# Column products of the FFN and MLP: two matrix instructions merged into one of 512 columns, the row factor applied at the residual

## What is computed

```
rms_norm(h, g) = h * rsqrt(mean(h * h) + eps) * g        # a factor per row, a gain per column
MLP:  h = h + square(relu(rms_norm(h, g) @ w_in)) @ w_out          # hidden width 4096, 2 times
FFN:  gate, up = split(rms_norm(h, g) @ w_gate_up)                 # hidden width 2816, 8 times
      h = h + 0.5 * ((silu(gate) * up) @ w_down)
```

## Time and profile before

| | before |
|---|---|
| three runs | 2901.33, 2904.25, 2906.99 us |
| median | 2904.25 us |
| span of the profiled execution | 2897.5 us |
| TensorE busy (matmul) | 2740.8 us, 95% |
| VectorE busy | 1697.9 us, 59% |
| ScalarE busy | 1285.5 us, 44% |
| mean granted TensorE clock | 0.969 |

### The profile page before, as it was taken

The page is one execution under the profiler, slowest core; times in us unless marked ns, Lnnn a source line. Parts: engine busy times, 40 slices in busy tenths (PEclk is TensorE's granted clock), DMA queues, the critical chain, the costliest instruction groups (busy, mean ns, idle before and its releaser), DMA issues.

```text
span 2897.5 us, 44300 instructions
## 1 busy us (share of the span) xinstructions
PE 2740.8 (95%) x18332; PEld 2491.1 (86%) x18342; DVE 1697.9 (59%) x1903; ACT 1285.5 (44%) x1376; POOL 6.8 (0%) x17
## 2 busy tenths in 40 slices
PE   7899998998999989999988999999799999998998
PEld 6689886997999869999976799999679999986997
DVE  6665576656555546565555455655655565564555
ACT  5443454334434544443433434444444444355433
POOL 0000000000000000000000000000000000000000
PEclk9899998999999999999998999999899999998999
DMA  7245432554454325545432255454315545541452
GB/s 270 87 177 189 174 139 82 194 191 148 162 189 165 139 84 184 194 174 187 179 139 80 101 189 189 175 188 170 115 45 201 179 171 201 184 153 70 163 185 73
DMA packets 63473, 454.85 MB, mean 157 GB/s; under 512 B 7104, under 2 KB 7360, under 8 KB 8848
## 3 DMA queue, kind: packets, MB, share of 16 engines
q1 hardware_dynamic: 61920, 448.82, 42.7%
q0 software_dynamic: 1024, 3.51, 0.3%
q10 hardware_dynamic: 432, 1.13, 0.1%
HBM read 452.38 MB, written 1.05 MB: 156 GB/s over the span
## 4 chain that ended last, share of the span: by engine, by line
PE 87%; DVE 6%; ACT 4%; issue 1%; DMA 1%; SPq 0%; DVEq 0%; ACTq 0%
PE tb L226 14%; PE tb L229 14%; PE tb L228 14%; PE acc L257 11%; PE acc L258 10%; PE acc L259 10%; DVE w_lo L206 2%; PE acc L226 1%; PE acc L228 1%; PE acc L229 1%; ACT w_hi L199 1%; PE tb L634 1%; PE tb L288 1%; PE acc L664 1%; PE tb L632 1%
## 5 line engine op out<-in xcount | busy, mean ns | idle before, releaser
L206 DVE TENSOR_TENSOR w_lo<-raw,w_hi 128x2048 fp32r<-128x2048 f32 x426 | 973.8, 2290 | 477.6 <-ACT w_hi L199 477.6
L199 ACT ACTIVATE w_hi<-raw 128x2048 fp32r<-128x2048 f32 x426 | 811.6, 1910 | 582.6 <-PE tb L229 302.9
L226 PE MATMUL tb<-xT,w_hi 128*128 128x256 f32 x3520 | 1004.0, 285 | 15.0 <-DVE w_lo L206 12.4
L228 PE MATMUL tb<-xT,w_hi 128*128 128x256 f32 x3520 | 997.4, 283 | 0.0
L229 PE MATMUL tb<-xT,w_lo 128*128 128x256 f32 x3520 | 997.2, 283 | 0.0
L226 PEld LDWEIGHTS tb<-xT,w_hi 128*128 128x128 f32 x3520 | 676.4, 192 | 24.4 <-DVE w_lo L206 8.1
L228 PEld LDWEIGHTS tb<-xT,w_hi 128*128 128x128 f32 x3520 | 676.6, 192 | 4.5
L229 PEld LDWEIGHTS tb<-xT,w_lo 128*128 128x128 f32 x3520 | 676.6, 192 | 0.0
L257 PE MATMUL acc<-w_hi,cat 128*128 128x512 f32 x1152 | 453.1, 393 | 10.1 <-DVE cat L674 6.5
L258 PE MATMUL acc<-w_hi,cat 128*128 128x512 f32 x1152 | 450.7, 391 | 0.0
L259 PE MATMUL acc<-w_lo,cat 128*128 128x512 f32 x1152 | 449.4, 390 | 0.0
(11 more groups left out here) (260 smaller groups left out, 2427.3 us busy)
## 6 DMA issues: line engine op xcount, KB each, us to landing
raw<-in_stream SPq DMA_DIRECT2D x426, 1024.0 KB, 4.8
h<-in_x SPq DMA_DIRECT2D x2, 512.0 KB, 4.9
gain<-in_gains POOLq DMA_DIRECT2D x2, 512.0 KB, 9.3
xn<-in_gates POOLq DMA_DIRECT2D x2, 512.0 KB, 8.4
out<-xn SPq DMA_DIRECT2D x2, 512.0 KB, 2.7
cst<-in_consts ACTq DMA_DIRECT2D x1, 960.5 KB, 12.5
big<-in_pT POOLq DMA_DIRECT2D x2, 256.0 KB, 3.0
gain<-in_gains POOLq DMA_DIRECT2D x1, 320.0 KB, 3.6
```

Source lines behind the costliest of these rows:

```text
L199: act.activation(w_hi[:, k % SPLIT, :], raw[:, k % RAW, :], ACT.Copy).then_inc(hi_done, 1)
L206: dve.tensor_tensor(w_lo[:, k % SPLIT, :], raw[:, k % RAW, :], w_hi[:, k % SPLIT, :], ALU.subtract).then_inc(lo_done, 1)
L226: pe.matmul(dst(f), hi, src[:, kt, 0, :], start=kt == 0 and (after is None or f == 0), stop=False, skip_group_check=after is not None)
L228: pe.matmul(dst(f), hi, src[:, kt, 1, :], start=False, stop=False, skip_group_check=after is not None)
```

## The change

`up` keeps high and low input side by side (they lie so in `xT`). For each tile and step it issues one instruction of 512 columns, high weights times both inputs, and one of 256 columns, low weights times the high input, behind the first half: two instructions where there were three. Each tile now has a PSUM bank of its own, high products in columns 0 to 255, low ones in 256 to 511, so a chunk fills two banks. ScalarE copies the second half out of both banks (new), VectorE adds it to the first half (in the MLP this add takes the place of the product with `rb`; in the FFN both sums are new, the gate is then still multiplied by `rb`, the up half no longer). The row factor of the up half, or its square in the MLP, goes into `residual` as a factor per row, with the 0.5. There is no second set of banks: TensorE waits for the sum of a pair before it overwrites its banks, and the first chunk of a phase goes to `acc` banks 0 and 2, so `zero_acc` now waits for the first sum.

```diff
-        def up(pe, c, bank, i=0, after=None):
-            columns(pe, c, lambda f: tb[:, bank, f * SEQ:(f + 1) * SEQ], 2, KT, SEQ, i, after=after)
+        def up(pe, c, banks, i=0, after=None):
...
+            for f, kt in order:
+                at = kt * SEQ + f * P
+                hi, lo = w_hi[:, s, at:at + P], w_lo[:, s, at:at + P]
...
+                both = xT[:, kt, :, :].rearrange("p a t -> p (a t)")
+                if kt == 0:
+                    pe.matmul(banks[f], hi, both, start=True, stop=False)
+                last = pe.matmul(banks[f][:, 0:SEQ], lo, xT[:, kt, 0, :], start=False, stop=False)
+                if kt:
+                    last = pe.matmul(banks[f], hi, both, start=False, stop=kt == KT - 1)
+            last.then_inc(chunk_used, 1)
+
+        UP_FIRST = [acc[:, 0, :], acc[:, 2, :]]
+        UP_0, UP_1 = [tb[:, b, :] for b in (0, 1)], [tb[:, b, :] for b in (2, 3)]
...
         def mlp_pe(pe, l, c, n):
-            up(pe, c, 0, after=x_ready(pe, n))
+            up(pe, c, UP_FIRST, after=x_ready(pe, n))
             if l == 0:
                 pe.wait_ge(*when("zeroed", 0))
+            pe.wait_ge(hid_v, base + 1)
             zero_acc(pe, c)
-            spread(pe, n)
...
-                    up(pe, c + 1 + 2 * j, (j + 1) % 3, i)
+                    pe.wait_ge(hid_v, base + 1 + j + 3 * i)
+                    up(pe, c + 1 + 2 * j, UP_0, i)
...
         def mlp_dve(dve, l, c, n):
...
-                by_rb(dve, two(f_up), two(tb[:, k % 3, :]), n, k == 0).then_inc(hid_u, 1)
+                dve.wait_ge(hid_b, bb + 1 + k + 3 * i)
+                dve.tensor_tensor(two(f_up), up_part(k or None, 0, 0), two(f_bu), ALU.add).then_inc(hid_v, 1)
...
         def ffn_pe(pe, f, c, n):
-            up(pe, c, 0, after=x_ready(pe, n))
-            zero_acc(pe, c)
-            up(pe, c + 1, 1)
-            spread(pe, n)
+            up(pe, c, UP_FIRST, after=x_ready(pe, n))
+            up(pe, c + 1, UP_1)
+            spread(pe, n, 0)
+            pe.wait_ge(hid_p, bg + 1)
+            zero_acc(pe, c)
+            pe.wait_ge(*when("rb", n))
...
+                    pe.wait_ge(hid_p, bg + 1 + j + 2 * i)
+                    up(pe, c + 2 + 3 * j, UP_0, i)
+                    pe.wait_ge(hid_v, base + 1 + j + 2 * i)
+                    up(pe, c + 3 + 3 * j, UP_1, i)
...
         def ffn_act(act, f, c, n):
...
+            low_gate(0, 0)
             split_hi(act, c, SPLIT)
-            hidden(0)
+            low_up(0, 1)
             split_hi(act, c, 1 + SPLIT)
+            spread_act(act, n, "ffn")
+            gate(0)
+            hidden(0)
...
         def ffn_dve(dve, f, c, n):
...
                     split_lo(dve, c, 3 + 3 * j + SPLIT, i)
+                    hidden_lo(j + 1, i)
+                    split_lo(dve, c, 4 + 3 * j + SPLIT, i)
...
-            residual(dve, n, c + CHUNKS_FFN - 1, 0.5)
+            residual(dve, n, c + CHUNKS_FFN - 1, row_scale)
...
-                    if last_kind != "bridge":
+                    if last_kind not in ("bridge", "ffn"):
                         split_lo(dve, c, -2 + SPLIT)
```

More of the change, by code:

```diff
@@ L186, in write @@
         cf = small[:, 226:228]
+        row_scale = small[:, 236:238]
         dots = small[:, 228:232]
@@ L328, in spread_act, with spread @@
         def spread_act(act, n, kind):
-            if kind not in ("ple", "bridge", "end"):
+            if kind not in ("mlp", "ple", "bridge", "end"):
                 act.wait_ge(*when("spread", n))
-                act.activation(rb, tb[:, 3, 0:SEQ], ACT.Copy).then_inc(*sig("rb", n))
-        def spread(pe, n):
+                act.activation(rb, tb[:, 0 if kind == "ffn" else 3, 0:SEQ], ACT.Copy).then_inc(*sig("rb", n))
+        def spread(pe, n, bank=3):
             pe.wait_ge(*when("diag", n))
-            pe.matmul(tb[:, 3, 0:SEQ], every, diag, start=True, stop=True).then_inc(*sig("spread", n))
+            pe.matmul(tb[:, bank, 0:SEQ], every, diag, start=True, stop=True).then_inc(*sig("spread", n))
         def newton(dve, root, mean, a, b, out_, key):
@@ L368, in factor_dve @@
             newton(dve, rms, ms, r0, r1, rstd, n)
+            if kind == "mlp":
+                dve.tensor_tensor(row_scale, rstd, rstd, ALU.mult).then_inc(*sig("own", (n, "scale")))
+                dve.wait_ge(*when("own", (n, "scale")))
+            if kind == "ffn":
+                dve.tensor_scalar(row_scale, rstd, 0.5, None, ALU.mult).then_inc(*sig("own", (n, "scale")))
+                dve.wait_ge(*when("own", (n, "scale")))
             if kind == "ple":
                 dve.nop().then_inc(*sig("rstd", n))
+            elif kind == "mlp":
+                pass
             elif kind not in ("bridge", "end"):
@@ L395, in x_ready, with residual @@
             return after
-        def residual(dve, n, c_last, scale=1.0):
+        def residual(dve, n, c_last, scale=None):
             for nn in range(2):
@@ L426, in down @@
                  acc_done=c if last else None, before_last=before_last)
-        def up(pe, c, bank, i=0, after=None):
-            columns(pe, c, lambda f: tb[:, bank, f * SEQ:(f + 1) * SEQ], 2, KT, SEQ, i, after=after)
+        def up(pe, c, banks, i=0, after=None):
+            pe.wait_ge(lo_done, c + 1 + RAW * i)
+            s = c % SPLIT
+            order = [(f, kt) for f in range(2) for kt in range(KT)]
+            if after is not None:
+                order.sort(key=lambda step: step[1])
+            for f, kt in order:
+                at = kt * SEQ + f * P
+                hi, lo = w_hi[:, s, at:at + P], w_lo[:, s, at:at + P]
+                if after is not None and f == 0:
+                    after(kt)
+                both = xT[:, kt, :, :].rearrange("p a t -> p (a t)")
[5 more added lines that the diff above has]
+            last.then_inc(chunk_used, 1)
```

117 lines of the change are left out of this document (72 added, 45 removed).

## The result

| | before | after |
|---|---|---|
| runs | 14 | 14 |
| median | 2903.20 us | 2910.02 us |
| lowest to highest | 2897.75 to 2906.99 us | 2907.80 to 2913.39 us |
| span of the profiled execution | 2897.5 us | 2911.6 us |

The ratio is 1.002, 95% interval 1.0013 to 1.0028: slower by 0.2%, 6.8 us, where 7 us faster was forecast. The time lies in the range and on the wrong side of no change.

A forecast was written before the change was run, and what follows sets the result against it. TensorE's pace was taken to bound the ten phases, other engines counting only at phase ends. A 43.3 us gain against waits of 11.2, 15.2 and 9.6 took 2904.25 to 2897 us, range 2884 to 2920.

The forecast's parts named there:

- The three waits: TensorE waits: 1.6 us at 7 FFN ends, 1.9 us at 8 FFN starts, 5.2 us idle at 2 MLP starts.
- the last pair's hidden low part: FFN end: ready about 5.6 us after its column product, wanted after 5.4; the 0.2 us lies under the residual wait.
- the sum: Whole kernel: -43.3 gain, +11.2 FFN ends, +15.2 FFN starts, +9.6 MLP starts, together -7.3 us.
- No wait inside the loops: Steady pairs in the loops: new copies and adds cost nothing more; TensorE waiting for sums there would show the forecast wrong.
- B: FFN starts: the clock falls at each, about 1.6 us more per FFN, 12.8 us, giving 2910 us; chance 0.14.
- C: Column products: a narrow instruction costs less behind a wide one, step 0.340 us, gain 66.6 us, time 2874 us; chance 0.08.
- the clock in the MLP: MLP starts: lower clock after the idle time loses 1.5 us each, bounds 0 and 2.5, 2 times.
- Gain 0.013 us a step, 43.3 us: Column products through `up`: 3328 steps lose one instruction each, a step falling from 0.360 to 0.347 us.
- columns plus 0.013: Matrix instructions at full clock: time is the columns' time plus 0.013 us, so 0.2267 us for 512 columns.
- D: Column products: the wide instruction on `xT` costs more than in the row product; slower, 2930 or 2963 us; chance 0.12.
- the estimate from it: Removed instructions: 2.5 ns fixed part each gives back 8.3 us, time 2932 us; no chance beyond D's.
- the first case: Whole kernel: the sum holds within its bounds, 2890 to 2903 us; chance 0.60.

The follow-up runs named there:

- the second profile: The changed kernel profiled once more with no edit, on one chip; 2910.35 us.
- The side by side: The kernel before and the changed kernel, each profiled once more with no edit and compared stage by stage; 2903.86 and 2910.35 us.
- the grouped kernel: Against the changed kernel with all three border moves: in each tile eight wide instructions first, then eight narrow ones; 2872.09 us, ratio 0.9884.

## Why the prediction was wrong

**What held.** The bound (TensorE's pace, other engines only at the borders). The three waits at their three places, from their causes: 1.30 us for 1.6, 1.74 for 1.9, 5.36 for 5.2. The first looks short because TensorE comes to it late: it has lost 0.26 us before on the last pair's hidden low part, which the forecast counted within its 1.6. From the last but one row product to the transposes it is 11.26 us, 9.55 before: 1.7 us in all. Taken away together the waits give 38.3 us by the medians and 36 by the ratios, where 36.0 stood in the sum; singly 10.9 for 11.2, 17.5 for 15.2, 13.5 for 9.6. No wait inside the loops. B did not happen, nor C.

For the clock in the MLP 1.5 us was taken out of bounds of 0 and 2.5. In the MLP shown the lower clock lasts from 163.20 to about 168.9 us, and there 4.4 us hold some seven steps that take 2.4 at full clock: 2.0 us, with 0.4 more for the zero instructions. This is the worst of four: in the second profile the same MLP is back at 0.35 us a step by 166.34, and it takes 186.7 us in place of 188.1; the second MLP takes 186.5 and 186.6. So the loss is 2.4 us once and about 1 us three times, after waits of the same length.

**What failed** is the first term of the sum, "Gain 0.013 us a step, 43.3 us". Measured alone it is 37 to 39.5 us. By the rows a step is 0.3494 and not 0.347 us: 3328 x 0.0024 = 8 us of the 43.3 were not there. Some 2.5 us came back at a place that the sum doesn't have: a row product starts without long intervals behind a chunk that ends on a wide instruction, and takes 5.444 us in place of 5.467, 110 times. The working took 0.2267 for the wide instruction by the rule "columns plus 0.013" and set the long intervals of the earlier trace rows aside as "the early intervals of that stretch". The change brings such intervals into every step: nearly all wide ones now take 231 to 241 ns, the narrow ones 113 to 120. The loss lies in the first tile of each chunk (0.3525 a step); the second, with the same two widths in turn, runs at 0.346 to 0.347, as forecast. So it is not a price for each change of width, but of one of two patterns that the order of widths brings about; the forecast itself said that 512 and 256 columns in turn "have no row at all", and gave that no price. Its bounds for the gain, 40 to 67 us, came from uniform stretches and single seams and lie wholly above 37 to 39.5. With the measured gain and the measured waits the sum is about -1 us, by the medians (-39.5 + 38.3) and by the ratios (-37 + 36) alike: no change.

**What was missing.** Some 6 to 8 us have no term in the sum. It was taken for certain that stages whose instructions are not touched stay as they are, and that the new structure costs nothing beside its waits. The side by side has the untouched stages at +4.8 us, and the kernel with narrow instructions and no waits is 0.22% above before. The three pieces as measured are -37 to -39.5 (pace), +36 to +38.3 (waits) and +6 (the new structure with neither), about +5 us, against 6.8; this closes by its making, since each kernel differs from the next by one piece, and is told for the sizes. Of the 6, some 3.5 us are placed, at the two ends of the FFNs. Why the attention phases take longer behind the changed kernel is not settled: their clock is lower, but the short phase of 35.7 us takes 37.3 in the first profile of the kernel before as well, and the untouched stages vary by 8 us over the 14 profiles, so how much of it is chance can't be told from these. It was not tried further.

**The rivals.** D had the right sign, and the step came to lie at its break-even of 0.349, but its reason was another: it asked whether `xT` makes the wide instruction longer (397 ns on it, 390 to 393 in the row product: it hardly does; in the grouped kernel eight on `xT` behind their like take 0.2263 each). C saw something real, a narrow instruction behind a wide one takes 113 to 120 ns, but the wide one behind it takes longer by as much or more. What it added at its end, that the two widths in turn have no row, was the nearer. The Trainium skill's page "TensorE: Matmul & The Clock Gate", section "Back-to-back issue gap", gives the 2.5 ns for a single matmul in isolation; the estimate from it made the gain 8.3 us and the time 2932 us, 22 us too high. The runs disagree with it for these float32 instructions: the measured 37 us are 11 ns for each removed one. The trace agrees with it for the four zero instructions alone, bf16 of 512 columns, whose starts lie 0.216 us apart.

**The chances.** Of 2897 us the forecast said itself that it lay just outside what can be told from no change. With a gain of 43 and costs of 36, each known to some 10%, a difference of 7 us was no more than its own uncertainty; 0.45 for faster was too much and 0.25 for slower too little. The bounds of the first case allowed for an error common to all steps on the side of a larger gain only. That the time lies in the stated range says little: the sum was 14 us off.

## What to carry to other kernels

A change that removes 3300 instructions gained 37 us and gave back as much in the order of a few instructions at the phase borders: after adding copies and sums to in-order engines, list for each border what now stands ahead of the operation that TensorE waits for, and move it behind; three such moves here make 0.2% slower into 1.05% faster. A new mix of instructions can't be priced from the old one's steady stretches, and its seams only bound it: a wide instruction behind a narrow one takes 233 ns there, a narrow one behind a wide one 114 and then 119, which leaves a step anywhere between 0.347 and 0.352 us, a gain between 43 and 27. Where two terms of forty microseconds nearly cancel, forecast "no difference" and measure each of them by a kernel of its own.

## What the hardware showed beyond that

- **The order of widths sets the pace.** With a weight load for each, 256 columns take 0.120 us and 512 take 0.2267 among their like. After narrow ones the next five wide ones take 233, 236, 228, 232 and 231 ns, 26 ns in all. In strict alternation a step takes 0.3533 us or 0.3470, by what ran before. For the same two instructions a step takes 0.348, 0.349 or 0.353 us on average by their order alone. Why is open.
- **At the lower clock the fixed part vanishes.** There a step takes 0.64 us (166.35 to 166.99), and 768 columns at 1.2 GHz are 0.640 us; in the kernel before, 256 columns take 213 ns at that clock (131 intervals), so three are 0.64 us as well. So the change gains nothing where the clock is low: the 13 ns are TensorE's at full clock only.
- **The fixed part differs by type.** At full clock 512 columns of float32 take 0.2267 us, and the zero instructions, 512 columns of bf16 (all zeros) with a weight load each, 0.216. Their weight loads take 0.10 us, those of the float32 ones 0.19; whether that is the reason was not tried.
- **A start of a program is not repeatable to 0.1%.** The first mixer, the same instructions in all kernels, ends between 143.3 and 148.4 us in the 14 profiles; in the pair before and after as first profiled this is 5 of the 14.1 us between the spans. Spans of single profiles are compared only after such a stage has been laid beside its like.
